# Attention loop of a hybrid decoder block: the copy of transposed probabilities moved ahead of the exponential, and the turn back of the sums moved by one step

## What is computed

```
h = rms_norm(x);  z = h @ w_in
q, k, v of 8 heads (2 KV heads, head width 64), gates, and the gMLP halves zu, zv come out of z
o_cmp = softmax over 31 compressed blocks
o_sel = softmax over selected blocks  (with 512 tokens all 8 blocks are selected: causal attention)
o_win = softmax over a window of 512  (with 512 tokens: causal attention on its own keys and values)
o_attn = g0 * o_cmp + g1 * o_sel + g2 * o_win
o_mix  = gelu(zu) * (spatial mix of rms_norm(gelu(zv)) + bias)
x = x + concat(rms_norm(o_attn), rms_norm(o_mix)) @ w_out
x = x + square(relu(rms_norm(x) @ w_ff1)) @ w_ff2
```

## Time and profile before

| What | us |
|---|---|
| Median of 3 runs | 648.05 |
| Lowest and highest | 646.58 and 649.35 |
| The profiled execution | 650.14 |
| Its span on the core | 648.1 |
| TensorE busy in the span | 591.6 |
| VectorE busy | 445.4 |
| ScalarE busy | 368.2 |

### The profile page before, as it was taken

One profiled execution on the slowest core, in us unless ns is written; L12 is line 12 of the kernel. 1 busy time (PEld: TensorE's weight loads), 2 busy tenths in 40 slices (PEclk: granted clock), 3 DMA queues, 4 the chain that ended last, 5 costly groups with the idle time before them and its releaser, 6 DMA issues.

```text
span 648.1 us, 9227 instructions
## 1 busy us (share of the span) xinstructions
PE 591.6 (91%) x3433; PEld 512.8 (79%) x3433; DVE 445.4 (69%) x725; ACT 368.2 (57%) x654; POOL 120.5 (19%) x198
## 2 busy tenths in 40 slices
PE   8999999998776765668899999999999999999998
PEld 7776877886665654557789999999998888888886
DVE  4798944865556445545478676755769998789774
ACT  7756635475455454564467635965359756556551
POOL 1630000013222221232103211022102303210100
PEclk9999999998878888888799999999999999999999
DMA  8823455331112001100029978599688979958872
GB/s 316 294 67 130 130 194 195 106 123 33 33 40 75 17 0 34 32 2 1 1 65 181 193 189 203 162 189 184 179 207 139 191 200 182 206 169 222 203 219 98
DMA packets 25164, 87.56 MB, mean 135 GB/s; under 512 B 3024, under 2 KB 3312, under 8 KB 25120
## 3 DMA queue, kind: packets, MB, share of 16 engines
q0 software_dynamic: 9856, 35.38, 29.5%
q1 hardware_dynamic: 15120, 51.59, 23.4%
q10 hardware_dynamic: 144, 0.00, 0.0%
HBM read 84.87 MB, written 2.10 MB: 134 GB/s over the span
## 4 chain that ended last, share of the span: by engine, by line
PE 70%; DVE 13%; ACT 7%; issue 6%; DMA 2%; SPq 1%; ACTq 0%; DVEq 0%
PE ps L425 20%; PE ps L427 20%; PE ps L426 20%; ACT pt_sb L1046 3%; DVE ps L1491 3%; DMA raw<-in_w 2%; ACT p_sb L1038 2%; DVE pt_sb L1515 2%; DVE xs L1545 1%; PE ps L1776 1%; PE ps L2049 1%; PE ps L1919 1%; PE ps L2068 1%; DVE w_lo_sb L1189 1%; DVE w_lo_sb L1185 1%
## 5 line engine op out<-in xcount | busy, mean ns | idle before, releaser
L1020 ACT ACTIVATE w_hi_sb<-raw 128x1024 fp32r<-128x1024 f32 x112 | 118.6, 1060 | 115.0 <-PE ps L427 90.3
L1553 DVE TENSOR_TENSOR w_lo_sb<-raw,w_hi_sb 128x1024 fp32r<-128x1024 f32 x112 | 136.9, 1224 | 64.6 <-ACT w_hi_sb L1020 64.3
L656 POOL DMA_DIRECT2D raw<-in_w_ff x64 | 55.2, 863 | 248.5 <-DVE w_lo_sb L1553 224.8
L425 PE MATMUL ps<-w_hi_sb,ht_hi 128*128 128x512 f32 x192 | 83.9, 437 | 13.4 <-DVE xs L1545 10.8
L426 PE MATMUL ps<-w_lo_sb,a_hi 128*128 128x512 f32 x224 | 87.2, 389 | 0.0
L425 PE MATMUL ps<-w_hi_sb,a_hi 128*128 128x512 f32 x224 | 87.2, 389 | 0.0
L427 PE MATMUL ps<-w_hi_sb,a_lo 128*128 128x512 f32 x224 | 87.2, 389 | 0.0
L425 PE MATMUL ps<-ht_hi,w_hi_sb 128*128 128x256 f32 (+1 forms) x272 | 79.2, 291 | 0.0
L427 PE MATMUL ps<-ht_hi,w_lo_sb 128*128 128x256 f32 (+1 forms) x272 | 78.9, 290 | 0.0
L426 PE MATMUL ps<-ht_lo,w_hi_sb 128*128 128x256 f32 (+1 forms) x272 | 78.8, 290 | 0.0
L1515 DVE TENSOR_TENSOR pt_sb<-ps,pt_sb 128x128 fp32r<-128x128 f32 (+3 forms) x64 | 31.4, 491 | 66.6 <-ACT pt_sb L1046 66.6
(11 more groups left out here) (237 smaller groups left out, 1191.7 us busy)
## 6 DMA issues: line engine op xcount, KB each, us to landing
raw<-in_w_ff POOLq DMA_DIRECT2D x64, 512.0 KB, 6.2
raw<-in_w_ff SPq DMA_DIRECT2D x48, 512.0 KB, 4.2
raw<-in_w SPq DMA_DIRECT2D x23, 512.0 KB, 4.5
xs<-in_x SPq DMA_DIRECT2D x8, 512.0 KB, 7.0
raw<-in_cmp_w SPq DMA_DIRECT2D x8, 512.0 KB, 4.4
xT<-in_xt SPq DMA_DIRECT2D x3, 512.0 KB, 8.8
raw<-in_w_c SPq DMA_DIRECT2D x4, 304.0 KB, 2.9
out_y<-xs SPq DMA_DIRECT2D x2, 512.0 KB, 3.2
```

Source lines behind the costliest of these rows:

```text
L425: pe.matmul(out, l_hi, r_hi, start=start, stop=False)
L656: pool.dma_start(raw[:, n % RAW, :], (w_ff1, w_ff2)[stage - 1][k, q], accum_op=ALU.add, max_dma_last_dim=8192).then_inc(raw_added[n % RAW] ...
L1020: act.activation(w_hi_sb[:, FS[j], :], raw[:, j, :], ACT.Copy).then_inc(w_hi, 1)
L1553: dve.tensor_tensor(w_lo_sb[:, FS[j], :], raw[:, j, :], w_hi_sb[:, FS[j], :].bitcast(F32), ALU.subtract).then_inc(w_lo, 1)
```

## The change

ScalarE does `pt_high(s)` ahead of `exp(w)` in each step of its loop. `BACK` is 2 where it was 1: `turn_back(i)` stands at step 4i + 7 of TensorE's loop, not 4i + 6, and `combine` one step later in VectorE's. `turn_back` had waited for `ot_keep(i)` in front of the next pair's first values. Now it stands behind them, so `values` itself waits for `ot_keep` of the pair before, at the first group of each pair.

```diff
 LAG = 2
-BACK = 1
+BACK = 2
 PB = 4
...
                 s = w - LEAD
                 job_act(ENDS.get(s))
+                if s < NV:
+                    pt_high(s)
                 if w < NV:
                     exp(w)
-                if s < NV:
-                    pt_high(s)
                 if s >= LAG and (s - LAG) % 4 == 3:
                     ot_keep((s - LAG) // 4)
...
                 pe.wait_ge(pt_lo, v + 1)
-                if i >= 2:
-                    pe.wait_ge(ot_evac, i - 1)
+                if i and (b == 0 or not t):
+                    pe.wait_ge(ot_evac, i)
                 out = ps[:, 6, i % 2 * 256:i % 2 * 256 + 256]
```

## The result

The changed kernel takes 605.76 us, the median of 4 runs (604.6 to 607.24). The kernel before took 648.04 in its 4 runs. The ratio is 0.9349, 95% interval 0.9318 to 0.9381: 42.3 us went, where 36 were forecast. The profiled execution took 606.64 us for a span of 604.6. One execution in experiment 5 had a lower granted clock and took 693 us; the ratios leave it out.

A forecast was written before the change was run, and what follows sets the result against it. ScalarE and VectorE working in turn were taken to bound the attention loop; TensorE's 125 us, less 11 for clock, plus 16 for pauses and 6 for meshing, gave 136 us, 36 less, so 612 us, range 597 to 631.

The forecast's parts named there:

- Loop 125 - 11 + 16 + 6 = 136 us: Attention loop: TensorE's work, less clock gain, plus remaining pauses, plus imperfect meshing; 36 us go from 172.
- the clock: TensorE in the loop: shorter pauses bring back half of the 22 us lost at the low clock, 11 us.
- The floor of 103 us: TensorE's work in the loop if all of it ran at the high clock, about 103 us.
- The pauses for adds: TensorE's waits in the loop for VectorE's adds into xs: half of the 15.7 us stays, 8 us.
- the other 31.1: TensorE's remaining idle time in the loop, including the 7.2 us for ot_sb: a quarter stays, 8 us.
- The plain step: Loop steps at 512 columns: 1.6 to 2.2 us each, where the step shown before took 2.68.
- The turn back and the wait in values: TensorE's loop: moving the turn back adds no gain of its own; the wait costs nothing, upper bound 15 us.
- The square root: ScalarE behind a norm root: the high part's copy comes before the exponential's table load and loads none; counted as nothing.
- A: Loop: TensorE keeps its low clock and most pauses; 21 us go, 627 us; chance 0.22.
- B: Loop: the clock comes back wholly and only 12 us of pauses stay; 51 us less, 597 us; chance 0.10.
- C: Loop: no change, freed time becomes waits for scaled probabilities; needs about 10.7 us per four steps; chance 0.04.
- D: Loop: exponentials miss their place before GpSimd's next pair, four steps take 11.9 us; 19 us slower, 667; chance 0.04.

The follow-up runs named there:

- experiment 5: The kernel before with two tiny four-column copies added on ScalarE behind every exponential of the loop; ratio interval 1.0131 to 1.0192, 10.4 us slower.
- Experiment 1: The kernel before with only ScalarE's order swapped, high part ahead of exponential; 603.36 us, ratio 0.932.
- experiment 3: The kernel before with ScalarE's old order, but scores and row maxima made five steps ahead instead of four; 604.8 us, ratio 0.9346.
- experiment 7: The kernel before with 16 useless transposes on TensorE in front of 14 job starts where it waits for adds; 644.69 us, ratio 0.9961.
- experiment 11: The kernel before with the swap, scores and maxima five steps ahead, old turn back, and VectorE's add ahead of the low part; 590.11 us, ratio 0.9112.
- Experiment 2: The kernel before with only the later turn back, combination and wait in values, ScalarE's order old; 646.36 us, ratio 1.0.
- experiments 9 and 10: The changed kernel and the swap alone, measured again side by side on one chip; 605.48 us, ratio 0.9354, against 603.08 us, ratio 0.9312.
- experiment 4: The changed kernel with scores and row maxima made five steps ahead as well; 596.21 us, ratio 0.9215 against the kernel before.

## Why the prediction was right

**The bound.** The two engines that work in turn were the bound of the loop, not TensorE with its 91%. Experiment 1 shows it by opening the loop, experiment 3 by opening it elsewhere with the same result, and experiment 5 by its price: 91% of what was added to ScalarE came out at the end. The prediction held that in stretches such as 295 to 300 nothing could go, because TensorE was busy 5.00 of 5 us; experiment 7 shows that stretch with TensorE idle 0.75 us at full clock, so the limit there was largely the low clock that the pauses had left.

**The sum.** Loop 125 - 11 + 16 + 6 = 136 us; it took 129.3. The idle time of TensorE was forecast at 22 us (16 for pauses, 6 for imperfect meshing) and measured at 20.8. That term was right. The term that was mis-sized is the clock: half of the 22 us at the low level, 11, where 16.7 came back (125.2 to 108.5). The floor of 103 us was sound: in experiment 11, with the clock at 1.00 through the whole loop, TensorE is busy 102.8.

The Trainium skill ("TensorE: Matmul & The Clock Gate", Part 1: The HAM clock gate) has the array at half rate after idling. Experiment 7 agrees: the same kernel with its pauses filled has a granted clock of 0.94 instead of 0.84.

**The pauses for adds.** Half of the 15.7 us were to stay, and 9.0 did. Of the other 31.1 a quarter was to stay and 6 us for meshing to be added, 13.8; measured are 20.8 - 9.0 = 11.8. One part came out 1 us too low and the other 2 too high, so that their sum fits this well is partly luck: the shares of a half and a quarter were estimates that no row gave.

**The plain step.** 1.6 to 2.2 us was forecast for 512 columns, on the ground that TensorE would be the pace. Five of the twelve distances are 1.95 to 2.21 us, in the range or at its edge. The pair shown takes 1.40 us, nearly VectorE's own 1.35, because VectorE was catching up. The average of the last stage, 38.1/16 = 2.4 us, holds the jobs with their waits.

**The turn back and the wait in values.** Both at nothing. Experiment 2 confirms it in the old order (ratio 1.0). The wait in values is as good as nothing: TensorE waits there 0.4 us in one place. But beside the swap the three parts together, turn back, combination and wait, cost 2.4 us (experiments 9 and 10). The prediction looked at who uses the combined rows and found them in time. It did not ask what the combination, one step later, would stand in front of on VectorE: that is the last reciprocal, and 0.78 us. So the whole gain is the swap's, and the second half of the change takes a little of it back.

**The square root.** The high part now comes straight behind it, and ahead of the load for the next exponential. ScalarE's timeline in the changed kernel:

```profile
248.15 1.28 ACT L757 ACT_TABLE_LOAD   x1
249.45 0.29 ACT L757 ACTIVATE rstd<-ssq,eps_sb 128x1 f32<-128x1 f32 x1
249.65 0.58 ACT L1046 ACTIVATE pt_sb<-ps 128x512 fp32r<-128x512 f32 x1
250.25 1.28 ACT L1038 ACT_TABLE_LOAD   x1
```

The copy at 249.65 has no load before it. The Trainium skill ("ScalarE: Activation LUTs", Table sets: the hidden batching unit) says that cheap functions such as copy are in every table set. The trace agrees.

**The rivals.** A (low clock and pauses stay) fell: the clock rose to 0.96. B (everything comes back, 597 us) was not reached by the change; experiment 4 reached it with a second cut. C and D needed a loop of 10.7 or 11.9 us through GpSimd for four steps; the time refutes them, and TensorE's wait for scaled probabilities stayed at 3.5 us.

## What to carry to other kernels

Where two engines each wait long for the other, write down the loop of one step and ask for each wait whether what is waited for could be made while the other engine works. Here it didn't matter which of two links was cut, and the second cut paid again (596 and 594 us, after 604). A wait that vanishes from the list while the loop stays as it is can come back as its neighbour's, as TensorE's 7.2 us did in experiment 2. A low granted clock of TensorE can be a consequence: repaired by itself it gave 2.5 us here. And a piece of work that is moved should be checked not only against those who wait for its result, but also against what it now stands in front of on its own engine.

## What the runs showed of the hardware

Two copies of four columns that follow each other read 0.19 us each in the profile, yet a pair takes 0.19 us of ScalarE's time from start to next start. So these copies start some 0.10 us apart and overlap by half, and their price is the distance of starts and not the duration. The table loads of 1.28 us were followed at once by the next instruction: 1.30 us from the start of the load to the next start (248.15 to 249.45), and the instruction before the load had ended at 248.13.
